# Two weight buffers of a fused transformer kernel begin 32 bytes later in each partition

## What is computed

```python
x = x + gla_mixer(rms_norm(x), w_in, ..., w_out)             # gated linear attention, 4 heads
x = x + swiglu(rms_norm(x), ffn_w_gu, ffn_w_down)            # hidden width 5632
h = h + concat(nsa_attention(...), stick_breaking(...)) @ w_out
h = h + memory_attention(rmsnorm(h), rmsnorm(mem), ...)      # 4 heads over 256 memory rows
# peer: 8 heads choose 16 of 16384 experts each, for every token
h = h + peer_ffn(rmsnorm(h), peer_w_q, sub_keys, peer_u, peer_v)
return rmsnorm(h, norm_final)

def token_block(xb, eb, gb):                                 # the gathers of peer_ffn
    a = einsum('td,ted->te', xb, u_tab[eb])
    return einsum('te,ted->td', gb * gelu(a), v_tab[eb])
```

## The kernel before

| tensor | before | mod 64 |
|---|---|---|
| rows, ring (each slot 8192 bytes) | 16512 | 0 |
| WH (4 x 4096) | 49280 | 0 |
| WL (4 x 4096) | 65664 | 0 |
| HL, HH (16384 each) | 82048, 98432 | 0 |
| XR, the residual | 114816 | 0 |
| rstd (holds the diagonals) | 141216 | 32 |
| arena, and so Y, A, N, MN, MO, DENSE_H | 145312 | 32 |

## Time and profile before

### The profile page before, as it was taken

The page is one execution under the profiler, slowest core; times in us unless marked ns, Lnnn a source line. Parts: engine busy times, 40 slices in busy tenths (PEclk is TensorE's granted clock), DMA queues, the critical chain, the costliest instruction groups (busy, mean ns, idle before and its releaser), DMA issues.

```text
span 3083.2 us, 34652 instructions
## 1 busy us (share of the span) xinstructions
PE 2723.6 (88%) x12212; PEld 1969.0 (64%) x12212; DVE 2111.9 (68%) x2870; ACT 1146.2 (37%) x1980; POOL 988.0 (32%) x567
## 2 busy tenths in 40 slices
PE   9999999999999999999999975666666877669997
PEld 8888788888887888999889872222223433235433
DVE  5687665555564545445566688887888887679877
ACT  5455555555553335445665530000002330034000
POOL 0021000000000000000000038777778777878864
PEclk9999999999999999999999997898999888988999
DMA  7444455555555555453354459999999999999997
GB/s 271 151 155 164 173 178 183 189 190 190 190 177 191 184 185 183 178 182 135 127 191 173 164 228 415 419 409 410 408 417 411 416 407 402 420 376 383 409 402 305
DMA packets 123586, 827.89 MB, mean 269 GB/s; under 512 B 22167, under 2 KB 22183, under 8 KB 23855
## 3 DMA queue, kind: packets, MB, share of 16 engines
q0 software_dynamic: 79392, 510.36, 40.8%
q1 hardware_dynamic: 43920, 313.73, 28.5%
q10 hardware_dynamic: 144, 2.10, 0.2%
HBM read 892.00 MB, written 4.22 MB: 291 GB/s over the span
## 4 chain that ended last, share of the span: by engine, by line
PE 58%; POOL 14%; DMA 11%; DVE 9%; issue 5%; ACT 3%; DVEq 0%; SPq 0%; ACTq 0%
PE ps L608 49%; POOL rows L1324 14%; DMA rows<-peer_u,arena 7%; PE ps L1230 2%; DMA rows<-peer_v,arena 2%; DMA rows<-peer_v 2%; DVE arena L2449 2%; PE ps L1241 2%; DVE WL L506 1%; PE ps L716 1%; ACT arena L1800 1%; DVE arena L209 1%; DVE arena L202 1%; PE ps L916 0%; DVE arena L203 0%
## 5 line engine op out<-in xcount | busy, mean ns | idle before, releaser
L506 DVE SCALAR_TENSOR_TENSOR WL<-ring,PA,WH 128x512 fp32r<-128x512 f32 x896 | 633.1, 753 | 461.7 <-ACT WH L490 445.1
L1241 PE MATMUL ps<-rows,rstd 128*128 128x512 f32 x1164 | 629.6, 694 | 300.1 <-DMA rows<-peer_v,arena 216.9
L2449 DVE CUSTOM_DVE_ANT_0 arena<-rows,arena 128x2048 f32<-128x2048 f32 x256 | 586.9, 2293 | 155.7 <-DMA rows<-peer_u,arena 128.9
L1241 PEld LDWEIGHTS ps<-rows,rstd 128*128 128x128 f32 x1164 | 245.8, 221 | 670.5 <-issue 371.9
L1324 POOL DMA_INDIRECT rows<-peer_v,arena x256 | 484.0, 1891 | 196.8 <-DVE arena L2449 73.4
L489 ACT ACTIVATE WH<-ring,PA 128x512 fp32r<-128x512 f32 x448 | 324.2, 724 | 550.1 <-PE ps L608 401.7
L1324 POOL DMA_INDIRECT rows<-peer_u,arena x256 | 451.4, 1763 | 165.7 <-DVE WL L506 85.9
L608 PE MATMUL ps<-WH,HH 128*128 128x512 f32 x1120 | 442.8, 395 | 4.0 <-DVE WL L506 4.0
L608 PE MATMUL ps<-WH,HL 128*128 128x512 f32 x1120 | 438.0, 391 | 0.0
L608 PE MATMUL ps<-WL,HH 128*128 128x512 f32 x1120 | 437.9, 391 | 0.0
L490 ACT ACTIVATE WH<-ring,PA 128x512 fp32r<-128x512 f32 x448 | 317.2, 708 | 0.0
(11 more groups left out here) (367 smaller groups left out, 3538.0 us busy)
## 6 DMA issues: line engine op xcount, KB each, us to landing
ring<-stream SPq DMA_DIRECT2D x292, 1024.0 KB, 4.8
rows<-peer_v POOLq DMA_DIRECT2D x32, 1024.0 KB, 15.4
rows<-peer_u,arena POOLq DMA_INDIRECT x256, 14.8
rows<-peer_v,arena POOLq DMA_INDIRECT x256, 15.0
arena<-xT SPq DMA_DIRECT2D x4, 512.0 KB, 9.3
bias_rows<-bias_scratch POOLq DMA_DIRECT2D x1, 2048.0 KB, 10.5
arena<-xT ACTq DMA_DIRECT2D x1, 2048.0 KB, 9.5
arena<-memT POOLq DMA_DIRECT2D x1, 2048.0 KB, 10.7
```

The lines of the kernel that those rows point to most:

```text
L506: ins = nc.vector.scalar_tensor_tensor(out=half_tile(WL, u)[:, s], in0=raw_half(u)[:, s], scalar=gain[d], in1=half_tile(WH, u).bitcast(f32 ...
L1241: last = mm(ps[:, 4 * tt + q, :], DIAG[:, k % DIAGS, :], rows[:, SLOTS[n % ROWS], q * CH:(q + 1) * CH], start=n == mine[0], stop=n == ends[q])
L2449: ins = V.tensor_tensor_reduce(out=JUNK, in0=rows[:, SLOTS[n % ROWS], :], in1=HN[:, tt, :], scale=1.0, scalar=0.0, op0=ALU.mult, op1=ALU.a ...
```

## The change

A slot of `ring` and `rows` becomes 2064 numbers long, 8256 bytes, of which 2048 are used as before. WH and WL each keep to two slots and begin 32 bytes into them. HL and HH begin at their slots' starts. What follows moves up by 768 bytes. To make room in the arena three scratch tiles go elsewhere: GE (the compressed blocks' GELU) lies over the small weights GWH and AGH, which are read out by then, and CA and EQ (the expert choice's candidates) lie over the first half of rstd. The instructions of every engine, their order and their waits are the same as before; only addresses differ, and the names of those three tiles.

| tensor | after | mod 64 |
|---|---|---|
| rows, ring (each slot 8256 bytes) | 16512 | 0 |
| WH | 49568 | 32 |
| WL | 66080 | 32 |
| HL, HH | 82560, 99072 | 0 |
| XR | 115584 | 0 |
| rstd | 141984 | 32 |
| arena | 146080 | 32 |

```diff
@@ -38,6 +38,9 @@
 ROWS = 12
+SLOT = TILE + 16
+PAIR = 2 * 4 * SLOT
+W_SHIFT = 32
 GROUPS = TT * PEER_H
@@ -235,15 +238,18 @@
-        rows, _ = place("rows", [P, ROWS, D])
-        ring, at = place("ring", [P, RING, TILE], at=at)
-
-
-        WH, at = place("WH", [P, UNITS, UNIT], f32r, at)
-        WL, at = place("WL", [P, UNITS, UNIT], f32r, at)
-        HL, at = place("HL", [P, KD, TOK], f32r, at)
-        HH, at = place("HH", [P, KD, TOK], f32r, at)
-        XR, at = place("XR", [P, TT, D], at=at)
+        rows_all, end = place("rows", [P, ROWS, SLOT])
+        rows = rows_all[:, :, 0:D]
+        ring_all, at = place("ring", [P, RING, SLOT], at=at)
+        ring = ring_all[:, :, 0:TILE]
+
+
+        WH, _ = place("WH", [P, UNITS, UNIT], f32r, at + W_SHIFT)
+        WL, _ = place("WL", [P, UNITS, UNIT], f32r, at + PAIR + W_SHIFT)
+        HL, _ = place("HL", [P, KD, TOK], f32r, at + 2 * PAIR)
+        HH, _ = place("HH", [P, KD, TOK], f32r, at + 3 * PAIR)
+        XR, at = place("XR", [P, TT, D], at=end)
+        GE, _ = place("GE", [P, 4, 4 * N_CMP], at=at)
@@ -331,7 +337,6 @@
-        GE, a = take(a, 4, 4 * N_CMP)
@@ -362,8 +367,8 @@
-        CA, _ = take(a, 256)
-        EQ, a = take(a, 2, 16, 16)
+        CA = rstd[:, 0, :]
+        EQ = rstd[:, 0:2, :].rearrange("p a (b c) -> p a b c", c=16)
```

## The result

The changed kernel takes 3097.03 us, median of five runs (3088.98 to 3098.23), against 3086.67 for the kernel before in the same comparison (3081.02 to 3088.2): 1.0041 times, 95% interval 1.0028 to 1.0054. Run again twice beside other kernels it gave 1.0051 (1.0030 to 1.0072) and 1.0030 (1.0018 to 1.0043). So it is slower, by about 0.4%; the forecast was no change, with 0.2 for slower.

A forecast was written before the change was run, and what follows sets the result against it. The matmul stream was taken to bound the first half, row-slot traffic the second. Terms -11.2 + 21.8 - 12.2 + 0.6 = -1.0 us, 94% counting, gave 3083.2 - 0.9 + 4.6 = 3086.9 us; range 3060 to 3114.

The forecast's parts named there:

- The bound and the halves: Whole kernel: first half bound by the stream of fp32r matmuls, second by filling and emptying row slots.
- Item 1: HH and HL stationary, W moving, 512 columns: 3360 matmuls at -3.33 ns, -11.2 us; bounds +22.4 and -22.4 us.
- Item 2: W stationary, HH and HL moving, 256 columns: 3264 matmuls at +6.67 ns, +21.8 us; lower bound -10.9 us.
- Item 3: Arena operands stationary, W moving, 512 columns: 1824 matmuls become like (0,0), -6.67 ns each, -12.2 us.
- Item 4: MN moving, W stationary: 192 matmuls, +3.33 or +6.67 ns each, +0.6 or +1.3 us.
- The slots: Row and ring slots 64 bytes longer: taken as 0 us, bound 8 us either way in the second half.
- The rival for it: Second half's transfers gain from slots starting at multiples of 256 bytes: 8 us, 3079 us; chance 0.03.
- Distance costs, whichever operand is off: Matmuls with W against HH and HL, both widths, pay 6.67 ns: +30 us, 3118 us; chance 0.17.
- weights 32 off cost nothing in the 256-column form: W stationary, HH and HL moving: 0 or -10.9 us, other gains remaining, 3056 to 3066 us; chance 0.26.
- The rule against any effect: TensorE: the skill's separate ports for weight loads and moving reads mean no placement matters; time exactly as now.
- VectorE, ScalarE and the three small tiles: 896 instructions on WH, WL and the ring, plus GE, CA and EQ: 0 us, tiles some tenths either way.

The follow-up runs named there:

- micro1: Stream-only kernel, the computation left out, one operand pair at a time: 512 columns 226.7 ns at distance 0, 233.3 at +32; 256 columns 120.0 and 116.8.
- arena_0: Kernel before with the arena 224 bytes later, at W's place modulo 256, three small tiles moved to make room: 3072.68 us, ratio 0.9961.
- shift_alone: Kernel before with WH and WL 32 bytes later, slots kept at 8192 bytes, two gaps of 256 bytes: 3086.36 us, ratio 1.0011.
- stagger_only: Changed kernel with WH, WL, HL and HH all 128 past a multiple of 256, longer slots kept: 3074.18 us, ratio 0.9975; again 0.9983.
- unshift: Changed kernel with the 32 bytes of WH and WL taken back, longer slots and moved scratch tiles kept: 3076.19 us, ratio 0.9978; again 0.9983.
- arena_32: Kernel before with 32 bytes of padding ahead of rstd, so rstd and the arena begin at a multiple of 64: 3082.59 us, ratio 1.0003.
- w_64: Kernel before with WH and WL 64 bytes past HL, HH and the arena modulo 256, slots of 8192 bytes with gaps: 3070.12 us, ratio 0.9962.

## Why the prediction was wrong

**The bound and the halves** were read rightly: the first half is a stream of three-product matmuls, the second the traffic of row slots, and the two moved on their own.

**Item 1 failed.** The prediction priced HH and HL stationary, W moving 32 bytes off, by the nearest row, rows 7, because there too the moving operand alone was off: -3.3 ns, -11.2 us. It measured +6.6 ns, +22 us. Rows 7 differed from the case in width as well, and the width was what counted: 32 bytes apart, 512 columns lose and 256 gain (micro1). The step behind it is "the excess is the same for 256 and 512 columns, so it belongs to one matmul with its weight load and not to its length": that was read from two rows at distance 0, 13.3 ns over both times, and at distance 32 the excess is 20.0 ns at 512 columns and 10.1 to 11.6 at 256. One of item 1's three products is moreover 96 bytes apart and not 32, which costs the same (234.3 ns in micro1).

**Item 2 failed in the same way, with the sign turned.** Form T was priced by rows 6, +6.67 ns, +21.8 us; it measured -1.1 ns, -3.6 us. The bounds given for both items held the true values: +6.67 and -3.33 to +6.67. The choice between the ends went by the side that is off, where "the form decides and not the side" stood there as the bound's reason. Two terms that were wrong by 33 and 25 us nearly cancelled: -11.2 + 21.8 against +22.2 - 3.6, +10.6 and +18.6 us. So the forecast lay much nearer to the result than its reasoning, by luck. What is left of the two errors, 8.0 us, and the 8.4 us of item 3 are what turned the forecast of no change into a loss; neither decides alone.

**Item 3 was right as a mechanism and mis-sized.** "If only the distance counts, they become like (0,0)" is what arena_0 and shift_alone show, 227.0 ns in the mean. But the change did not bring all three products to distance 0. WL stands 16512 bytes behind WH, 128 modulo 256, so WL and the arena are 128 apart. The prediction's residues modulo 64 could not show it. It brought 2 ns, -3.8 us, in place of -12.2. By the table, two products at 226.7 and one at 232.4 to 233.5 would be 228.6 to 229.0 ns; three profiles of the changed kernel gave 231.4, 232.7 and 231.2 in the mean. That remainder is not explained.

**Item 4**: +2.4 ns each, +0.5 us, about as forecast.

**The slots were mis-sized at 0.** The bound of 8 us either way was about right and the effect real: stagger_only gains 8.4 us behind form T in its first profile, the changed kernel 5.5 over three. The rival for it had the mechanism and the size (8 us), and a chance of 0.03. A rule with a price in it, about the very thing the change does and a stretch where the DMA engines are 98% busy, deserved more. "The engines already run full" was an argument for the effect, not against it.

**The rivals.** "Distance costs, whichever operand is off" is what happened for the 512 columns of item 1 and the arena. Its 3118 us failed by form T, which it had paying 21.8 us; "weights 32 off cost nothing in the 256-column form" had that half. The two were put as alternatives, and the truth was the first half of one with the second of the other: 22.2 - 3.6 - 3.8 + 0.5 = +15 us, and less the slots' gain some 3093 to 3097 us, inside the range of 3060 to 3114.

**The rule against any effect.** From the Trainium skill, TensorE: Matmul & The Clock Gate, Part 2, first step (the load of the next weights takes no read bandwidth from the running matmul), the prediction had drawn that no placement should matter. That conclusion is refuted for these fp32r pairs: with one load for each matmul, moving only the places gave 226.7 to 234.3 ns for the same 512 columns, and 113.3 to 120.0 for 256. Whether the page's sentence itself is wrong is not shown, since no run here separates the load of weights from the matmul; in unshift the next weights' place did not set the time at 512 columns. What memory structure makes 256 bytes the period was not tried; no run shows it.

**VectorE, ScalarE and the three small tiles** cost nothing that shows: the splitting instruction takes 753 ns as in rows 10, and kernels that differ in the small tiles' places alone beside one further edit (arena_0, stagger_only) come out as that edit's price.

## What to carry to other kernels

When a change moves buffers, write down for every pair of operands the distance of their starts modulo 256, not each start modulo 64, and take the price for a pair from a row of the same width: here 32 bytes cost 512-column matmuls 6.6 ns and saved 256-column ones 1 to 3. The table of single streams gave the kernel's intervals within about 1 ns in most cases, and missed by 2 to 5 ns in a few (the arena in the changed kernel, form T in unshift, MN in arena_32 and w_64), so check a planned layout in the trace. Before writing off a term because an engine is already full, ask whether the change makes that engine's own work shorter: a full engine is where a per cent on each packet is a per cent of the stretch. Both were worth more as a tuning knob than the change itself: row slots at multiples of 256 and W 64 bytes past its partners made the same instructions 0.8% to 1% faster than the kernel before.

## What was not expected of the hardware

- fp32r matmuls with one weight load each run at 226.7 ns for 512 columns at distance 0 and 232 to 234 at most others, +64 being a second good place (228.8) while -64 is not (233.3); for 256 columns 0 is the worst (120.0) and 64 either way the best (113.3). The same distance can be best for one width and worst for the other.
- Fewer stationary columns bring little at 512 columns: 16 take 231.2 to 231.7 ns and 64 take 230.0 to 231.6 at the three distances tried (0, +32, -32), more than 128 at distance 0 (226.7) and less than 128 at 32 (233.3). At 256 columns and distance 0, 64 take 113.3 ns and 16 take 120.0.
- With the queues full, a write of 8192 bytes into on-chip memory takes 309.0 ns where it begins at a multiple of 256, and 313 to 314 elsewhere, even at other multiples of 64 or 128. In the kernel the transfers' mean of 319.4 ns fell to 315.7, and over half of the gain came already with a quarter of the slots at such a start.
- Executions of one kernel scatter by up to 5 us ahead of the last form-T matmul and 6 behind it, over half the size of the whole effect here; the intervals between starts repeat to 0.2 ns in most kinds of pair. For a change of this size the intervals times the counts say more than two spans do.
